# A two-layer mixer with expert retrieval: the context's mixer of layer 0 ahead of the latents', one context expert tile gathered beside the latents' mixer of each layer

## The chip, the cores and the metric

The kernel runs on one core of a Trainium2 chip. The metric is the device time of one execution in microseconds (us); the time before is the median of three runs. All data are float32.

## What is computed

512 latent tokens and 256 context tokens, 1024 wide, pass through two layers. Cut to what matters here:

```
h, hc = modulated RMSNorm of the latents x and of the context xc
p, pc = h @ w_in, hc @ w_in                       # 12 column blocks of q, k, v; z; gates; branches
oc, s_f, s_b = delta rule over pc, both directions, from a zero state
o            = delta rule over p,  both directions, from the context's final states
x = x + gt1 * (concat(o gated by z, 2-D DFT branch, convolution branch) @ w_out)
x = x + gt2 * peer(norm(x))
if not last:                                      # the context is changed in layer 0 only
    xc = xc + cgt1 * (same with oc) ;  xc = xc + cgt2 * peer(norm(xc))

peer(h): 8 heads of product keys choose 16 experts each, 128 for a token;
         y = sum over the 128 of  weight * gelu(u[e] . h) * v[e]
```

The delta rule is worked in chunks of 64 tokens; for each tile a triangular system is solved by an inverse that is doubled level by level.

## The kernel before

Tokens go in tiles of 128, two of context and four of latents; an expert tile is one of them with its 128 slots. A slot is one indirect gather that GpSimd issues: 128 rows of 8 KB (u and v of one expert for each token), 1 MiB. VectorE takes the dot product of u and h, ScalarE gelu, weight and a diagonal matrix, TensorE adds diagonal times v into two PSUM banks (two matmuls for a slot, recorded as four of 512 columns), or VectorE adds weight times v itself.

The stages follow one another, each in a block with one queue of instructions for each engine, ordered by hand:

- Layer 0: `begin` (L153), `projection` (L420, all 768 columns, 18 chunks of weights in a ring of three, 64 dots for the modulation vectors of layer 1 among its VectorE work), `branches` (L1246), `gdn_tiles` (L1426, six tiles), `gdn_scan` (L1788, twelve steps), `mix_out` (L2164, six tiles and the scoring of the first), `peer` (L2455, five tiles: latents, then the first context tile; each tile's successor is scored beside it).
- Layer 1: `projection_latents` (L720), with the last context tile of layer 0 as the held tile (`HeldTile`, L291): all its 128 slots are gathered and summed here through a ring of six rows. Then `branches_beside_context` (L960), which also adds the held sum to the context and projects the context's keys and values, `gdn_tiles` and `gdn_scan` as in layer 0, `mix_out` and `peer` for four tiles.

So ten expert tiles are gathered: nine in `peer`, one held.

Of `gdn_tiles`, for a tile and each of five levels: GpSimd masks a block (L1765), TensorE multiplies (L1549), ScalarE copies (L1633), TensorE multiplies again (L1558, L1561), VectorE subtracts (L1700). The next tile's start (L1658 to L1682) lies between the levels; behind the last level come two passes with the right sides (L1577, L1583) and their copies (L1713). The held tile's methods are called from the queues of a stage: `gathers` on GpSimd (L333), `dve` (dots L347, adds L369), `act` (L376, L379, L386), `pe` (L397). Its ring row is free for slot g + 6 when slot g is summed:

```python
def gathers(self, pool, upto):
    for g in range(self.issued, min(upto, SLOTS)):
        if g >= HELD_RING:
            self.free(pool, g - HELD_RING)
        self.gather(g)
```

In `peer` the same steps are L2585 (gather), L2606 (dot), L2733 to L2741 (ScalarE) and L2831 (TensorE). In `projection`, L524 and L527 are the matmuls of the latents' and the context's columns and L639 the modulation dots; in `projection_latents`, L779 are the latents' columns. In the scoring, L2093 to L2161 pick the experts on VectorE.

Of the kernel before, what the change touches and what calls it, by code (L numbers as in the profile page):

```python
# [10 lines left out]
P = 128  # L11
# [82 lines left out]
def lengths_of(kit):  # L94

    return kit.gw[:, 0, 0:NT * 2 * H].rearrange("p (t g) -> p t g", g=2 * H)
# [48 lines left out]
DOTS_FIRST, DOTS_EACH = 20, 1  # L145
# [7 lines left out]
def begin(nc, kit, hT, spare, ahead):  # L153
# [3 lines left out]
    with ExitStack() as mem, phase(nc, kit, "const_in", "prm_in", "cond_in", "cols_in", "cond_blank", "cond_silu", "cond_ready",  # L157
                                   "prod_ready", "ss_ready", "ms_ready", "root_ready", "xn_ready", "turned", "hT_ready",
                                   "row_copied", "row_turned", "cols_ready", "dve_step", *["x%d" % t for t in range(NT)],
                                   *["w%d" % k for k in range(KD)], in_flight=True) as (  # L160
            const_in, prm_in, cond_in, cols_in, cond_blank, cond_silu, cond_ready, prod_ready, ss_ready, ms_ready, root_ready,
            xn_ready, turned, hT_ready, row_copied, row_turned, cols_ready, dve_step, *ins):
# [18 lines left out]
        with nc.Block() as block:  # L181
            @block.sync
            def _(sp):
# [9 lines left out]
                ahead(sp)  # L193
                sp.wait_ge(prm_in, 16)

            @block.scalar
            def _(act):
# [22 lines left out]
                for k in range(KD):  # L220
                    for st in range(2 if on_act(k) else 0):
                        nc.scalar.activation(hT[:, k, sides[st]], hT[:, k, sides[st]], ACT.Identity,
                                             bias=shift[:, st, k:k + 1], scale=scale[:, st, k:k + 1])
# [30 lines left out]
            def _(dve):  # L254
# [23 lines left out]
                for k in range(KD):  # L278
                    for st in range(0 if on_act(k) else 2):
                        nc.vector.tensor_scalar(hT[:, k, sides[st]], hT[:, k, sides[st]], scale[:, st, k:k + 1],  # L280
                                                shift[:, st, k:k + 1], ALU.mult, ALU.add)
# [4 lines left out]
HELD_A_CHUNK = 6  # L286
HELD_A_ROW = 5
# [3 lines left out]
class HeldTile:  # L291


    BANKS = (1, 3)

    def __init__(self, nc, kit, L, j, sems, rows):
# [4 lines left out]
        self.rows = rows  # L301
        self.h, self.eid, self.gw = kit.hc[:, j % 2, :], kit.eid[:, j % 2, :], kit.gw[:, j % 2, :]
        self.table = kit.experts.rearrange("l e d -> (l e) d")
        TAPS_FROM, TAPS_TO = 6 * HELD_A_CHUNK, 18 * HELD_A_CHUNK
        spare = lambda g: g % 3 == 1 if TAPS_FROM <= g < TAPS_TO else g % 3 != 0
# [47 lines left out]
    def settle(self, dve):  # L353

        for g in range(max(self.dots - 2, 0), self.dots):
            self.add(dve, g)

# [54 lines left out]
PJ_RING = 3  # L412
# [7 lines left out]
def projection(nc, kit, L, first, hT, qkvT, zs, ab, fT, acc, w, w_in):  # L420
# [5 lines left out]
    whole = lambda c: first == 0 or NCV + H <= c < NCV + NQKV  # L426
    segments = lambda c: ((0, CTX), (CTX, T)) if whole(NCV + c) else ((CTX, T),)
    ROWS = SEQ // GRID_W
    W = GRID_W + 2 * HALO
# [3 lines left out]
    with ExitStack() as mem, phase(nc, kit, "mod_in", "mod_prod", "mod_rows", "mod_bias_in", "mod_stored", "wz_in", "proj_ready", "proj_read", "p_ready",  # L433
                                   "y_ready", "y_used", "rows_ready", "padded", "sq_ready", "sum_ready",
                                   "root_ready", "root_turned", "dve_step", "blank", "cond_in", "cond_ready", "dot_bias_in",
                                   "dotted", "dots_biased", "dots_turned", "dots_copied", "dots_stored",
                                   *["dw%d" % r for r in range(DOT_RING)]) as (
            mod_in, mod_prod, mod_rows, mod_bias_in, mod_stored, wz_in, proj_ready, proj_read, p_ready, y_ready, y_used, rows_ready, padded, sq_ready,
            sum_ready, root_ready, root_turned, dve_step, blank, cond_in, cond_ready, dot_bias_in,
            dotted, dots_biased, dots_turned, dots_copied, dots_stored, *dot_w):  # L440
        sb = lambda n, s: mem.enter_context(nc.sbuf_tensor(f"pj{n}_{L}", s, FP32))
        dot_rows = sb("dot", [P, DOT_RING, D])
        next_cols = sb("nx", [P, 2, len(DOTS)])
        next_rows = sb("nr", [P, P])
# [2610 lines left out]
```

## Time and profile before

| | us |
|---|---|
| median of three runs | 4368.07 (4365.26 to 4369.1) |
| span of the profiled execution | 4365.4 |
| layer 0, begin | 44 |
| layer 0, mixer (projection to output) | 628 |
| layer 0, peer, five tiles | 1637 |
| layer 1, mixer up to the scan, with the held tile | 610 |
| layer 1, scan and output | 143 |
| layer 1, peer, four tiles | 1302 |

The profiled execution's span lies 2.7 us below the median of the runs. Over the whole span TensorE is busy for 85%, VectorE 69%, ScalarE 39% and GpSimd 38%, and the DMA engines move 1506 MB. In the rows below, busy times are unions of an engine's instructions; a group's "idle before" is the engine's idle time just before its instructions, with what ended it; the DMA share is the mean busy share of the 16 DMA engines.

### The profile page before, as it was taken

Reading aid. Unit: us, or ns where it says so; the run is one execution under the profiler, and the core shown is the slowest. Engines: PE = TensorE matmul, PEld = TensorE weight load, DVE = VectorE, ACT = ScalarE, POOL = GpSimd, SP = SyncE. Lnnn points to the kernel's source line nnn. Section 1 sums busy time; section 2 is a strip of 40 time slices with the busy share of each in tenths; the row PEclk is TensorE's granted clock in tenths of the full one; section 3 lists DMA queues with packets and bytes.
Section 4 is the critical chain, followed back from the end, with each engine's and each line's share of the span. In section 5 each row is a group of like instructions: output and inputs, shape, how many; then the busy total and the mean of one; then the engine's idle time right before and its main releaser. Section 6 shows DMA issues by size and latency. Waiting matters only on the chain. (4 is left out here: it accounts for less than half of the span.)

```text
span 4365.4 us, 55131 instructions
## 1 busy us (share of the span) xinstructions
PE 3693.1 (85%) x18945; PEld 1903.6 (44%) x18945; DVE 3006.0 (69%) x6251; ACT 1720.2 (39%) x5270; POOL 1645.7 (38%) x1508
## 2 busy tenths in 40 slices
PE   7998998988888887888886888888898888888777
PEld 3566854533433433433432335775443343343222
DVE  3964666975775875875875885557797687687444
ACT  2223623444344344344342454353444433433333
POOL 0004513443443443444443432352444444444332
PEclk9999999999999999999998999899999999999999
DMA  8360159999999999999999997015999999999997
GB/s 336 122 239 29 37 198 367 416 421 421 418 415 422 414 417 421 407 420 422 410 412 369 408 394 303 2 37 190 404 422 421 421 421 421 421 413 421 422 421 325
DMA packets 238985, 1506.07 MB, mean 345 GB/s; under 512 B 28433, under 2 KB 33617, under 8 KB 71153
## 3 DMA queue, kind: packets, MB, share of 16 engines
q0 software_dynamic: 184320, 1342.26, 74.7%
q1 hardware_dynamic: 54384, 160.28, 9.9%
q8 instruction: 150, 2.46, 0.2%
q14 instruction: 131, 1.07, 0.1%
HBM read 1490.32 MB, written 12.12 MB: 344 GB/s over the span
## 5 line engine op out<-in xcount | busy, mean ns | idle before, releaser
L2831 PE MATMUL ps<-low,pediag 128*128 128x512 f32 x2180 | 1058.7, 615 | 226.1 <-ACT pediag L2741 219.3
L2606 DVE CUSTOM_DVE_ANT_0 low<-low,hc 128x1024 f32<-128x1024 f32 x545 | 667.8, 1225 | 359.3 <-DMA low<-in_experts_dram,eid 342.0
L2585 POOL DMA_INDIRECT low<-in_experts_dram,eid x539 | 595.0, 1104 | 812.4 <-PE ps L2831 783.2
L2733 ACT ACTIVATE low<-peact 128x1 f32<-128x1 f32 x1152 | 232.1, 201 | 1335.0 <-DVE peact L2606 1334.0
L2831 PEld LDWEIGHTS ps<-low,pediag 128*128 128x128 f32 x2180 | 388.9, 192 | 824.5 <-ACT pediag L2741 499.4
L2741 ACT ACTIVATE pediag<-cst,low 128x128 f32<-128x128 f32 x1152 | 462.5, 402 | 42.1 <-PE ps L2831 4.5
L2831 PE MATMUL ps<-wide_a,pediag 128*128 128x512 f32 x640 | 307.8, 612 | 54.4 <-ACT pediag L2741 54.2
L2736 ACT ACTIVATE low<-low,gw 128x1 f32<-128x1 f32 x1152 | 339.1, 294 | 37.4
L2831 PE MATMUL ps<-wide_b,pediag 128*128 128x512 f32 x640 | 303.3, 605 | 50.7 <-ACT pediag L2741 48.5
L2060 PEld LDWEIGHTS ps<-qkvT,arena 128*128 128x128 f32 x2560 | 312.0, 193 | 75.4 <-issue 75.4
L2060 PE MATMUL ps<-qkvT,arena 128*128 128x128 f32 x2560 | 313.1, 276 | 2.4 <-ACT qkvT L2024 2.4
L2606 DVE CUSTOM_DVE_ANT_0 wide_a<-wide_a,hc 128x1024 f32<-128x1024 f32 x160 | 196.2, 1226 | 97.3 <-DMA wide_a<-in_experts_dram,eid 91.2
L2606 DVE CUSTOM_DVE_ANT_0 wide_b<-wide_b,hc 128x1024 f32<-128x1024 f32 x160 | 196.2, 1226 | 96.9 <-DMA wide_b<-in_experts_dram,eid 91.4
L2585 POOL DMA_INDIRECT wide_a<-in_experts_dram,eid x158 | 169.8, 1074 | 237.4 <-PE ps L2831 232.7
L2831 PE MATMUL ps<-last_b,pediag 128*128 128x512 f32 x456 | 219.4, 608 | 46.2 <-ACT pediag L2741 44.9
L2831 PE MATMUL ps<-last_a,pediag 128*128 128x512 f32 x456 | 220.5, 612 | 43.0 <-ACT pediag L2741 41.6
L2585 POOL DMA_INDIRECT wide_b<-in_experts_dram,eid x158 | 176.2, 1115 | 195.8 <-PE ps L2831 188.5
L2831 PEld LDWEIGHTS ps<-wide_a,pediag 128*128 128x128 f32 x640 | 114.4, 193 | 227.1 <-ACT pediag L2741 134.8
L2831 PEld LDWEIGHTS ps<-wide_b,pediag 128*128 128x128 f32 x640 | 113.5, 189 | 217.5 <-ACT pediag L2741 120.5
L2606 DVE CUSTOM_DVE_ANT_0 low<-last_b,hc 128x1024 f32<-128x1024 f32 x114 | 139.7, 1225 | 80.9 <-DMA last_b<-in_experts_dram,eid 77.6
L2606 DVE CUSTOM_DVE_ANT_0 low<-last_a,hc 128x1024 f32<-128x1024 f32 x114 | 139.6, 1225 | 76.1 <-DMA last_a<-in_experts_dram,eid 72.2
L2585 POOL DMA_INDIRECT last_b<-in_experts_dram,eid x112 | 121.4, 1084 | 163.1 <-PE ps L2831 156.0
(497 smaller groups left out, 5773.9 us busy)
## 6 DMA issues: line engine op xcount, KB each, us to landing
pjdot<-in_mod_t_dram SPq DMA_DIRECT2D x64, 512.0 KB, 5.2
arena<-in_w_mod_dram SPq DMA_DIRECT2D x24, 1024.0 KB, 14.4
arena<-in_peer_wq_dram SPq DMA_DIRECT2D x8, 2048.0 KB, 17.1
low<-in_experts_dram,eid POOLq DMA_INDIRECT x609, 8.7
pjw<-in_w_cols_dram SPq DMA_DIRECT2D x18, 512.0 KB, 3.7
plw<-in_w_cols_dram SPq DMA_DIRECT2D x18, 512.0 KB, 8.1
x_rows<-low SPq DMA_DIRECT2D x10, 512.0 KB, 7.7
qkvT<-mod_rows SPq DMA_DIRECT2D x9, 512.0 KB, 7.6
```

The costliest lines, as they stand in the source:

```text
L2060: last = self.nc.tensor.matmul(self.kit.ps[:, 4 + q % 2, 0:P], self.kit.wq[:, i, q * P:(q + 1) * P], self.hT[:, i, :], start=i == 0, stop= ...
L2585: nc.gpsimd.indirect_dma_start(ring.row(g), None, table, bass.IndirectOffsetOnAxis(eid[:, j % 2, k:k + 1], 0)).then_inc(ring.landed(g), 16)
L2606: nc.vector.tensor_tensor_reduce(out=dot_out if final else ring.row(g)[:, 0:D], in0=ring.row(g)[:, 0:D], in1=hc[:, j % 2, :], scale=1.0, s ...
L2733: nc.scalar.activation(ge[:, g % 2, 0:1], act_v[:, j % 2, k:k + 1], ACT.Gelu_apprx_tanh).then_inc(gelu_ready, 1)
L2736: nc.scalar.activation(ge[:, g % 2, 1:2], ge[:, g % 2, 0:1], ACT.Copy, scale=gw[:, j % 2, k:k + 1]).then_inc(weighed, 1)
L2741: nc.scalar.activation(diag[:, g % DIAGS, :], ident, ACT.Copy, scale=ge[:, g % 2, 1:2]).then_inc(diag_ready, 1)
L2831: last = nc.tensor.matmul(ps[:, half, :], diag[:, g % DIAGS, :], ring.row(g)[:, D + half * 512:D + (half + 1) * 512], start=k == 0, stop=k ...
```

## The change

1. Layer 0's mixer runs for the context alone first, then for the latents. `projection` becomes `projection_context` (256 columns, eight weight chunks loaded ahead in `begin`, which also stores the latents' turned rows to memory); `branches` becomes `branches_context`; `gdn_tiles` takes a range of tiles, `gdn_scan` a range of steps. The 64 modulation dots (`ModDots`) are spread over these context stages: 6 and 12 in the projection, 14 in the branches, 20 in the delta-rule tiles, 12 in the scan.
2. A new stage `mix_context` makes the output projection of both context tiles, scores all eight heads of context tile 0 and starts its first six gathers.
3. That tile is the held tile of layer 0's latents: 48 slots beside `projection_latents` (two for each of 18 chunks, three for each of four rows of z), 16 beside `branches_latents`, 64 beside `gdn_tiles` (three for each of five levels and one more, for each of four tiles). One slot in three is added on VectorE, the others on TensorE. In `gdn_tiles`, TensorE and ScalarE run one level behind VectorE's dots. `gdn_scan` then does the latents' eight steps, `mix_out` the four latent tiles.
4. `peer` of layer 0 has four tiles; context tile 1 is scored beside the fourth, and its norm's square, turning and store come after the last slot. It is the held tile of layer 1, in the same three stages.
5. In layer 1 the context's rows, keys and values (`context_rows`) and its two delta-rule tiles, without outputs, follow as stages of their own behind the latents' `gdn_tiles`; the scan has twelve steps as before.
6. In `gdn_tiles` the gram and both kinds of differences share PSUM banks 0 and 1 and follow one another, since the held tile's sums take banks 2 and 3.

The core of the diff:

```diff
-DOTS_FIRST, DOTS_EACH = 20, 1
+DOTS_FIRST, DOTS_BRANCHES, DOTS_TILES, DOTS_SCAN = 6, 14, 20, 12
...
 HELD_RING = 6
 HELD_DIAGS = 3
-HELD_A_CHUNK = 6
-HELD_A_ROW = 5
+HELD_BEHIND = 2
+HELD_BRANCHES, HELD_TILE = 16, 16
...
-        spare = lambda g: g % 3 == 1 if TAPS_FROM <= g < TAPS_TO else g % 3 != 0
+        spare = lambda g: g % 3 == 1
...
-PJ_RING = 3
+PJ_RING = 8
...
+def gdn_tiles(nc, kit, L, lo, hi, outs, qk, low, gate, kt, us, wT, qkd, decs, dts, vt, work, held=None, dots=None):
...
+    HELD_LEVEL = 3
...
+            @block.tensor
...
+                for u in range(N):
                     for n in range(NL):
...
+                        if held and u + n:
+                            held.pe(pe, HELD_LEVEL)
+                    if u + 1 < N:
+                        turn_inverse(u + 1)
...
+                    if held:
+                        held.pe(pe, HELD_TILE - NL * HELD_LEVEL)
...
+            @block.scalar
...
+                            elif n == 1:
+                                decay_matrices(u + 1)
+                            elif n == 2:
+                                reach_matrices(u + 1)
                         if n == 3:
+                            decays(u)
+                        if held and u + n:
+                            held.act(act, HELD_LEVEL)
...
+            @block.vector
...
+                            nc.vector.tensor_tensor(both, both, updates(d, kinds), ALU.subtract
                                                     ).then_inc(upd_done, 1)
...
+                        if held:
+                            held.dve(dve, HELD_LEVEL)
+                        if dots:
+                            dots.dve(dve, DOTS_TILES // (N * NL))
...
+            @block.gpsimd
...
+                    if u:
+                        rows_for(HELD_LEVEL)
+                    block_of(u, 2)
+                    right_values(u, 0)
+                    if u:
+                        rows_for(HELD_LEVEL)
+                    block_of(u, 3)
+                    right_keys(u, 0)
+                    rows_for(HELD_LEVEL)
+                    block_of(u, 4)
+                    right_values(u, 1)
+                    rows_for(HELD_LEVEL)
+                    block_of(u, 5)
+                    if u + 1 < N:
+                        block_of(u + 1, 0)
+                    right_keys(u, 1)
+                    rows_for(HELD_TILE - 4 * HELD_LEVEL)
...
+def mix_context(nc, kit, o, mixT, zs, bufs_of, xb, w, held):
...
+                for h in range(PH):
+                    sc.pick(j, 2 * h)
+                    sc.pick(j, 2 * h + 1)
+                    sc.combine(h)
...
+                pool.wait_ge(sc.eid_ready, 1)
+                for g in range(HELD_RING):
...
+                    held.gather(g)
...
-                peer(nc, kit, 0, order, len(order) - 1, qkvT, ring, low[:, LOW_Y:LOW], held)
+            peer(nc, kit, 0, order + [NC - 1], len(order), flat, ring, low[:, LOW_Y:LOW], held)
...
+        context_rows(nc, kit, 1, ctx_qk, ab, gate, yacc, wide, kit.arena[:, PL_ROWS:PL_ROWS + 6 * D])
+        us_c, wT_c, kt_c = solved(PL_ROWS, NC)
+        gdn_tiles(nc, kit, 1, 0, NC, False, ctx_qk, low, gate, kt_c, us_c, wT_c, None, decs, dts, kit.hc[:, 1, :], wide[0])
```

## Rows read from the trace of the kernel before

**Rows 1.** Windows by stage: us, busy us of each engine, TensorE's clock, DMA share, GB/s.

```profile
45.00:300.00 255.00, 254.12 (x877) 150.34 (x877) 195.12 (x322) 45.26 (x83) 2.00 (x7) 0.99 0.57 209
300.00:345.00 45.00, 37.01 (x152) 16.91 (x152) 21.85 (x37) 17.58 (x31) 0.00 (x0) 0.99 0.63 246
345.00:501.00 156.00, 133.42 (x3760) 118.25 (x3760) 82.94 (x122) 58.10 (x171) 84.28 (x73) 0.94 0.01 3
501.00:555.00 54.00, 48.41 (x768) 42.44 (x768) 35.99 (x63) 44.97 (x146) 37.62 (x34) 1.00 0.20 71
...
673.00:2310.00 1637.00, 1386.85 (x4216) 651.56 (x4216) 1189.84 (x2677) 678.92 (x2197) 709.69 (x638) 0.99 1.01 416
2310.00:2690.00 380.00, 304.65 (x708) 135.26 (x708) 295.53 (x418) 161.00 (x410) 145.39 (x128) 0.93 0.96 378
2690.00:2765.00 75.00, 64.88 (x244) 43.79 (x244) 38.85 (x92) 32.10 (x59) 0.23 (x3) 0.90 0.34 127
...
2970.00:3063.00 93.00, 77.47 (x296) 43.84 (x296) 60.70 (x187) 17.70 (x62) 8.90 (x9) 0.92 0.69 256
3063.00:4365.00 1302.00, 1088.56 (x3080) 482.87 (x3080) 891.82 (x1923) 522.29 (x1698) 535.43 (x503) 0.99 0.99 411
```

**Rows 2.** Page, costliest groups: the dot of the expert stages.

```profile
L2606 DVE CUSTOM_DVE_ANT_0 low<-low,hc 128x1024 f32<-128x1024 f32 x545 | 667.8, 1225 | 359.3 <-DMA low<-in_experts_dram,eid 342.0
```

**Rows 3.** Groups by line, 45 to 300 us: columns, dots and their read.

```profile
L639 DVE CUSTOM_DVE_ANT_0 pjdot<-pjdot,hc 128x1024 f32<-128x1024 f32 x64 | 77.8, 1225 | 42.2 <-DMA pjdot<-in_mod_t_dram 30.9 <-ACT hc L601 10.0
L527 PE MATMUL ps<-low,pjw 128*128 128x256 f32 x288 | 65.1, 379 | 0.0
...
L639 DVE DVE_READ_ACCUMULATOR2_ANT pjnx<- 128x1 f32 x64 | 5.3, 82 | 0.0
```

**Rows 4.** Timeline of VectorE, 440 to 466 us: the levels' subtractions in `gdn_tiles`.

```profile
441.94 1.28 DVE L1700 TENSOR_TENSOR gdX<-gdX,ps 128x512 f32<-128x512 f32 x2 [3.21 <-PE ps L1561]
...
447.25 1.27 DVE L1700 TENSOR_TENSOR gdX<-gdX,ps 128x512 f32<-128x512 f32 x2
...
449.99 1.29 DVE L1700 TENSOR_TENSOR gdX<-gdX,ps 128x512 f32<-128x512 f32 x2 [0.87 <-PE ps L1561]
...
460.63 1.39 DVE L1700 TENSOR_TENSOR gdX<-gdX,ps 128x512 f32<-128x512 f32 x2 [0.63 <-PE ps L1561]
465.22 1.28 DVE L1700 TENSOR_TENSOR gdX<-gdX,ps 128x512 f32<-128x512 f32 x2 [3.21 <-PE ps L1561]
```

**Rows 5.** Window of the scoring of four heads in `mix_out`, columns as in Rows 1.

```profile
587.00:635.00 48.00, 47.86 (x201) 28.54 (x200) 40.81 (x142) 6.35 (x19) 2.05 (x2) 1.00 0.33 120
```

**Rows 6.** Held stage: its projection matmuls (by line), one slot's matmuls (timeline).

```profile
L779 PE MATMUL ps<-wide_a,plw 128*128 128x512 f32 x288 | 140.9, 620 | 20.0 <-DMA plw<-in_w_cols_dram 20.0
...
2506.73 1.88 PE L397 MATMUL ps<-low,parts 128*128 128x512 f32 x4
```

**Rows 7.** Line L2450 (first gathers in `mix_out`), from issue to landing.

```profile
DMA to landing us min/median/max: 6.4/6.6/6.9
```

**Rows 8.** Timeline of ScalarE, 2371 to 2378 us: table load, then one held slot.

```profile
2372.61 0.60 ACT L820 ACTIVATE arena<-ps 128x512 f32<-128x512 f32 x1
2373.22 1.28 ACT L376 ACT_TABLE_LOAD   x1
2374.51 0.20 ACT L376 ACTIVATE parts<-parts 128x1 f32<-128x1 f32 x1
2374.75 0.29 ACT L379 ACTIVATE parts<-parts,gw 128x1 f32<-128x1 f32 x1
2375.07 0.40 ACT L386 ACTIVATE parts<-cst,parts 128x128 f32<-128x128 f32 x1
```

**Rows 9.** Lines L1675, L2146, L333: durations min/median/max in ns, first and last start.

```profile
L1675 DVE TENSOR_TENSOR qkd<-qkd,cst x10: 817/1427/1659, 361.9 to 2894.4; 128x512 f32<-128x512 f32 x10
...
L2146 DVE TENSOR_TENSOR qkvT<-qkvT,mosif x8: 691/692/693, 607.5 to 3047.3; 128x512 f32<-128x512 f32 x8
...
L333 POOL DMA_INDIRECT arena<-in_experts_dram,eid x22: 933/940/1986, 2288.6 to 2673.9; - x22
```

More of the change, by code:

```diff
@@ L987, in branches_beside_context @@
-        w = lambda c: wa[:, c] if c < 5 else wb[:, c - 5]
+        gate_c, gain, sc, sh = (room[:, i * D:(i + 1) * D] for i in range(4))
+        xb = room[:, 4 * D:6 * D].rearrange("p (i n) -> p i n", n=D)
+        w = lambda c: weights[c // 4][:, c % 4 * KD * P:(c % 4 + 1) * KD * P].rearrange("p (k n) -> p k n", k=KD)
         hb = kit.hc
@@ L1307, in _ @@
+                dots.load(sp, dots.done + DOT_RING + DOTS_BRANCHES)
+                sp.wait_ge(mod_rows, MOD_GROUPS)
+                for j in range(MOD_GROUPS):
+                    sp.dma_start(mod_store(kit, 0, 2, j), row[32 * j:32 * j + 2, :]).then_inc(mod_stored, 16)
+                sp.wait_ge(mod_stored, 16 * MOD_GROUPS)
             @block.vector
@@ L1795, in gdn_scan @@
     ready_at = {}
-    for c in range(2 * first, NCH):
+    for c in range(S0, s_hi):
         s = max(step_of(d, c // 2, c % 2) for d in range(2))
@@ L2168, in mix_out @@
+def mix_out(nc, kit, L, tiles, o, mixT, flat, zs, w, ring):
     HALVES = 2 * len(tiles)
@@ L2210, in products_reading @@
                 return 1
-            here = [i for i in range(n_tiles) if tiles[i] // 2 == row - 4]
+            here = [i for i in range(n_tiles) if (tiles[i] - NC) // 2 == row - 4]
             return 2 * (max(here) + 1) if here else 1
@@ L2452, in _, with peer @@
                         bass.IndirectOffsetOnAxis(kit.eid[:, 0, g:g + 1], 0)).then_inc(ring.landed(g), 16)
-def peer(nc, kit, L, tiles, here, qkvT, ring, room, held):
+def peer(nc, kit, L, tiles, here, flat, ring, room, held):
     N, M = len(tiles), here
@@ L2961, in backbone @@
[L2961 to L2969 removed]
+        first_row = flat[:, 4 * D:6 * D]
@@ L2972, in constants @@
+        scan.close()
+        with phase(nc, kit, *["e%d" % r for r in range(RING + 2)], gathers=RING + 2) as sems:
+            ring = RowRing(first_row, ring_rows + [kit.cst[:, P:P + 2 * D]], [6, 8, 4, 5, 0, 1, 2, 3, 7], sems[0:RING + 2])
+            mix_out(nc, kit, 1, order, lat_o, lat_mix, flat, lat_z, half_weights, ring)
+            peer(nc, kit, 1, order, len(order), flat, ring, low[:, LOW_Y:LOW], None)
 def constants():
```

1780 lines of the change are left out of this document (986 added, 794 removed).

## The prediction

> **What bounds the kernel now.** I read the stage table first [rows 1]: one row for each stage of the program, with the busy time of each engine, the granted clock and the DMA share. The reader is to see two kinds of stage. In the two expert stages (673 to 2310 us, 3063 to 4365 us) the DMA share is 1.01 and 0.99 while TensorE is busy for 85 and 84%: nine tiles of 128 gathers of 1 MiB go through at 1637/5 = 327 us a tile, 2.55 us a gather. In a mixer stage it is the other way round: TensorE is busy nearly throughout, and the DMA share is 0.01 in layer 0's delta-rule stage and 0.20 in its scan. The one exception is the stage at 2310 us, where a whole expert tile is gathered beside the latents' projection (DMA share 0.96). VectorE's wait for the expert rows [rows 2] is what ends most of its idle time in the expert stages, so an expert tile taken out of them gives back its full price. The question is what the tile costs where it is put, and what it costs to split a mixer stage of six tiles in two.
>
> **What leaves the expert stages.** Layer 0 keeps four tiles in peer instead of five: minus 327. At its end the last context tile gets the norm, the turning and the store that lay beside another tile before, about 14 us with no cover (nothing to 20). Minus 313. Layer 1's expert stage keeps its instructions: 0.
>
> **The context's own mixer in layer 0, stage by stage.** Before, two context tiles ride along with four latent ones; the matmuls are already kept apart by stream, so columns cost the same, but each stage has a start, an end and weights of its own.
> Begin: four stores of the turned latents and five more weight chunks on SP's queue: plus 4 (0 to 8).
> Projection: TensorE alone has 65 us of 256-column matmuls [rows 3], a third of the z pass (15), the modulation products (16) and the wait for the first pieces: 97. VectorE has 18 dots of 1.225 plus 0.08 for the read of the sum [rows 3], 24 us, beside convolutions and taps, at 5.75 us a chunk over twelve chunks. I take 104 (95 to 115).
> Branches: the stage of six tiles lasts 45 [rows 1]; the Fourier products of the latents leave it, 14 dots (18 us of VectorE) and 8 MB of weights come in, at 2.52 us per MiB as in the expert stage 20 us. I take 42 (36 to 48).
> Delta-rule tiles: one tile lasts 23.3 us (441.94 to 465.22 [rows 4]), six of them 140, so 16 of the 156 [rows 1] are start and end. Two tiles: 46.6 + 16 = 63. Two dots (2.6 us) stand behind each of the ten levels' subtractions on VectorE, and the next subtraction queues behind them: the short levels grow from 2.74 us (447.25 to 449.99 [rows 4]) to 3.9, plus 7: 70 (64 to 76).
> Scan: 54 for twelve steps [rows 1], 4.5 a step; four of them 18, with twelve dots (16) and 8 MB of output weights and keys to land: 37 (30 to 42).
> Output and scoring: the held tile needs all 128 expert numbers before its first gathers, so all eight heads are scored with nothing beside them. Four heads take VectorE 40.8 us of 48 [rows 5], eight 82; ahead of them lie the 32 us from 555 to 587, and 5 behind: 119 (112 to 125).
> Sum 104 + 42 + 70 + 37 + 119 = 372, with 4 us between stages 376.
>
> **A held tile beside the latents' mixer, once per layer.**
> Projection with 48 slots: TensorE is busy 304.7 us in the stage of before [rows 1], with 67 slots summed on it and eight context chunks. A slot's four matmuls take 1.88 us in the stream [rows 6], a context chunk 65.1/18 = 3.6 [rows 3]. Two thirds of 48 slots are 32, so 304.7 − 8 × 3.6 − 35 × 1.88 = 210; TensorE sat idle for 20.0 before the first weights [rows 6]: 230 (220 to 245). It is a bound of TensorE, not of the gathers (48 × 2.55 = 122).
> Branches with 16 slots: between the 45 and the 75 that the two stages of before last [rows 1]: 59.
> Delta-rule tiles with 16 slots each: this is the term that decides, and no row of before shows it. Three slots follow each of a tile's five levels on VectorE; TensorE and ScalarE take them one level later; the ring has six rows, so three gathers are issued only when the three of two levels ago are summed. Follow one set of three round: a lone gather lands 6.6 us after its issue [rows 7], the two behind it 2.52 later each, 11.6; the last dot 1.2; gelu, copy and diagonal 0.20 + 0.29 + 0.40 [rows 8]; the matmuls 1.9: 15.6, and with the hand-overs about 16.4 for two levels, 8.2 a level against 2.74 to 5.3 now [rows 4]. Five levels 41; the passes behind the last level 5.2 (23.3 less 4.6 + 5.3 + 3 × 2.74); the sixteenth slot 2.5. ScalarE goes from gelu to exp and back three times a tile, six table loads of 1.28 us [rows 8], 7.7, half of it on the loop: 3.9. Together 53 a tile, 4 × 53 + 16 = 228. From below, a tile can't beat its TensorE work, 133.4/6 = 22.2 [rows 1] + 10.7 × 1.88 = 42, nor 16 gathers, 40: 172 to 184 for the stage. From above, a ring in which each level waits for the set before it (11.5 a level): 245.
> In [rows 8] the table load begins 0.01 us behind the activation ahead of it. The Trainium skill's page "ScalarE: Activation LUTs" (What ACT_TABLE_LOAD costs) adds a drain of about 1.38 us to each switch, 2.66 in all; by it a tile would take 4 us more and the two layers 33. No such gap shows in the rows, so the sum goes without it.
> Sum 230 + 59 + 228 = 517, with gaps 520. The scan of the latents 8 × 4.5 = 36.
>
> **The sums.** Layer 0's mixer: 376 + 520 + 36 + 93 (four tiles of output, as 2970 to 3063 [rows 1]) = 1025 instead of 628 (45 to 673): plus 397, with begin plus 401. Layer 1: 520, then the context's rows, keys and values by themselves (29 of TensorE, 59 with their loads and rows; 45 to 70), two context tiles without outputs (60), 2 of gaps: 641 instead of 610 (2310 to 2920): plus 31. Later stages: 0. Altogether 401 − 313 + 31 = plus 119 on a span of 4365.4, 4484.4. The median of the runs is 2.7 us above the span, so the forecast is 4487, plus 2.7%.
> In other words, splitting costs layer 0 some 220 us (two sets of starts and ends, the scoring that lost its cover), and a held slot costs (517 − 324)/128 = 1.51 us beside the mixer instead of 2.55 in peer; 324 is the same stage without slots (170 + 45 + 109). Gathers are hidden; matmuls, dots and the ring are not.
>
> **Rivals.**
> Faster, by one mechanism: TensorE's slack takes the slots. It is idle for 20 us at the head of the projection and 15% of the delta-rule stage, and its many 64x64 matmuls have modelled ends, so part of "busy" may be room. If a slot costs 0.85 us instead of 1.51, two layers win 256 × 0.66 = 169: 4318 (4280 to 4357 for 0.7 to 1.0). It decides below 1.51 − 119/256 = 1.04 us a slot. Against it: the held tile of before, where nothing else was short, cost (380 − 199)/128 = 1.41 a slot, and TensorE's two thirds alone are 1.25.
> Slower still: VectorE and GpSimd get in each other's way. The same 128x512 product of two SBUF operands takes VectorE 0.69 us where GpSimd does nothing and 0.82 to 1.66 in the delta-rule stages, where GpSimd works; and a gather's issue takes GpSimd 0.93 to 1.99 [rows 9]. Held dots are long operations of that kind, and the block masks that release each level are GpSimd's. If each level's mask waits out one dot (1.2) and three issues grow by 0.3, that is 2.1 for each of 20 levels, 42 a layer: 4487 + 84 = 4571 (4540 to 4640). The Trainium skill's "SBUF — State Buffer" (SBUF: two separate sides) has this as a lock: an operation of VectorE with two SBUF inputs and one of GpSimd that reads SBUF take turns, whole instructions at a time. The stretched rows agree; how often they meet beside a dot no row shows.
> No change: a slot at 1.0 to 1.08. That the gathers do not run beside the mixer at all (2.55 a slot, 4753) speaks against the stage at 2310 us, where they do.
>
> **How the numbers follow.** The forecast with its bounds (4420 to 4540: most of the unknowns are independent, the tiles' 172 to 245 the largest) 0.56; slower still 0.22; faster 0.17; within 0.2%, about what a measurement of this kernel can tell from no change, 0.05. The range leaves out the far ends of both rivals: 4340 to 4580. So faster 0.17, same 0.05, slower 0.78.
>
> **What would show it.** In the changed kernel's trace: layer 0's peer shorter by 313; context stages of about 376 ahead of the latents' projection, with 82 us of scoring on VectorE and a DMA share near 0 there; the delta-rule stages of four tiles at 53 us a tile, VectorE idle for expert rows and GpSimd for sums and adds; the projection of the latents TensorE-bound at 230. Wrong would be tiles of 42 us (the ring covers its latency), or context stages near 300. With both, the change gains.

## The result, and the profile after

The changed kernel takes 4646.2 us (median of four runs, 4639.6 to 4656.4) against 4368.4: 1.064 times the time before, with a 95% interval of 1.062 to 1.065. The direction was forecast, the size was not: plus 278 us instead of plus 119, and past the top of the range.

The profiled execution has a span of 4647.9 us, 282.5 above that of before. Laid out by stage, the answer to [rows 1], windows of the changed kernel (us, busy us of TensorE, its weight loads, VectorE, ScalarE, GpSimd, then TensorE's clock, DMA share, GB/s):

```profile
50.70:162.00 111.30, 99.06 (x436) 72.34 (x437) 69.35 (x141) 24.04 (x51) 0.81 (x6) 0.93 0.70 265
162.00:213.40 51.40, 21.66 (x96) 6.74 (x96) 29.02 (x63) 10.50 (x19) 0.00 (x0) 0.63 0.83 317
213.40:288.40 75.00, 54.17 (x1264) 47.27 (x1264) 55.04 (x82) 20.90 (x60) 33.41 (x25) 0.82 0.44 140
288.40:337.10 48.70, 23.97 (x257) 20.61 (x257) 29.63 (x48) 16.12 (x51) 12.30 (x10) 0.67 0.57 211
337.10:457.30 120.20, 69.12 (x368) 50.70 (x368) 87.92 (x299) 16.64 (x59) 5.82 (x7) 0.77 0.41 153
457.30:721.20 263.90, 231.40 (x568) 107.74 (x568) 144.46 (x212) 107.94 (x216) 54.99 (x52) 0.93 0.67 235
721.20:781.00 59.80, 46.38 (x100) 20.03 (x100) 39.91 (x69) 30.88 (x70) 19.63 (x16) 0.91 0.77 287
781.00:1034.00 253.00, 186.15 (x2680) 116.59 (x2681) 173.42 (x234) 108.67 (x305) 137.32 (x110) 0.88 0.71 257
...
1167.90:2487.90 1320.00, 1114.91 (x3408) 526.66 (x3408) 959.91 (x2172) 547.86 (x1772) 571.30 (x511) 0.98 1.00 414
2487.90:2752.20 264.30, 231.50 (x568) 107.76 (x569) 144.58 (x212) 107.94 (x216) 56.01 (x52) 0.93 0.66 235
...
2811.10:3075.80 264.70, 196.75 (x2680) 120.22 (x2680) 173.22 (x234) 108.64 (x304) 135.69 (x110) 0.84 0.68 247
```

The first five rows are the context's own stages of layer 0 (projection, branches, delta-rule tiles, scan, output with scoring), the next three the latents' stages with the held tile, then layer 0's four expert tiles, then the projection and the delta-rule stage of layer 1. Against the forecast:

| | forecast | measured | off by |
|---|---|---|---|
| begin | +4 | +5.8 | +2 |
| context's stages, layer 0 | 376 | 406.6 | +31 |
| held stages, layer 0 | 520 | 576.7 | +57 |
| scan and output of the latents | 129 | 133.9 | +5 |
| peer, layer 0 | −313 | −317 | −4 |
| held stages, layer 1 | 520 | 587.9 | +68 |
| context's rows and tiles, layer 1 | 121 | 126.5 | +5 |
| scan, output and peer, layer 1 | 0 | 0 | 0 |

Three quarters of the miss lie in the two times three held stages, most of the rest in the context's stages. Inside the held stages the branches came out as forecast (59.8 and 58.9 for 59), though not for the forecast's reasons (a_six below); the projections took 264 each instead of 230 and the delta-rule stages 253 and 265 instead of 228, each with the gap of 2 to 6 us behind it. From first to last instruction, as the stages are timed from here on, they are 262 and 263, 247 and 258.

What the engines wait for in layer 0's delta-rule stage, 781 to 1028 us (engine, line, awaited; us in total, times, longest):

```profile
PE ps L442 <- ACT parts L431: 51.5, 22, 4.7
...
DVE low L414 <- ACT parts L424: 21.9, 10, 5.1
DVE arena L382 <- DMA arena<-in_experts_dram,eid: 13.9, 9, 3.1
...
DVE wide_b L382 <- DMA wide_b<-in_experts_dram,eid: 9.6, 8, 2.0
DVE qkvT L382 <- DMA qkvT<-in_experts_dram,eid: 9.3, 5, 4.4
```

TensorE idles 51.5 us in front of held sums (L442), for their diagonals from ScalarE (L431). VectorE idles 33 us for expert rows and 22 for the weights of its adds. The forecast's loop, in which everything waits for rows, should show the rows first.

There are 22 such waits in the four tiles, of two main kinds. Six of them, 18.6 us together, are like this one; timeline of a level of the changed kernel (start us, duration us, engine, line; "..." stands for lines left out):

```profile
869.66 0.85 ACT L1600 ACTIVATE low<-ps 128x256 f32<-128x256 f32 x2 [4.83 <-PE ps L1502]
...
870.53 1.28 ACT L1574 ACT_TABLE_LOAD   x1
...
871.19 1.28 DVE L1676 TENSOR_TENSOR wide_a<-wide_a,ps 128x512 f32<-128x512 f32 x2 [3.90 <-PE ps L1514]
...
872.45 1.13 PE L1453 MATMUL ps<-low,cst 128*128 128x256 f32 x4
873.62 0.60 ACT L1574 ACTIVATE low<-ps 128x512 f32<-128x512 f32 x1 [1.81 <-PE ps L1453]
874.24 1.28 ACT L421 ACT_TABLE_LOAD   x1
...
876.09 0.40 ACT L431 ACTIVATE parts<-cst,parts 128x128 f32<-128x128 f32 x1
...
876.55 1.98 PE L442 MATMUL ps<-wide_b,parts 128*128 128x512 f32 x4 [2.96 <-ACT parts L431]
...
878.37 1.88 PE L442 MATMUL ps<-arena,parts 128*128 128x512 f32 x4
...
880.18 1.15 PE L1502 MATMUL ps<-wide_a,low 64*64 64x64 f32 x32
```

The subtraction of the level ends at 872.47 and TensorE's matmul for the next tile (L1453) at 873.58; then the next level's first pass (L1502) could start. It starts at 880.18. ScalarE has the next tile's exponential (L1574) ahead of the held slots; the exponential waits for that matmul of TensorE; behind it stands a table load for gelu; and TensorE, whose queue has the held sums ahead of the next pass, waits for the diagonal. The table load begins 0.02 us behind the exponential that ends at 874.22, and the gelu follows at 875.53. The Trainium skill's "ScalarE: Activation LUTs" (What ACT_TABLE_LOAD costs) states a drain of about 1.38 us beside each load; as in [rows 8], no such gap shows here.

The longest wait of each tile is of the other kind (4.2 to 4.7 us, 17.8 us in four):

```profile
829.04 1.28 ACT L1569 ACT_TABLE_LOAD   x1
...
830.34 0.21 ACT L1569 ACTIVATE decs<-gdsums 64x8 f32<-64x8 f32 x1
...
831.71 1.28 ACT L421 ACT_TABLE_LOAD   x1
...
834.44 2.08 PE L442 MATMUL ps<-arena,parts 128*128 128x512 f32 x2 [4.67 <-ACT parts L431]
```

Here ScalarE has eight short exponentials of the tile's own decays (L1569, L1570), which wait for nothing, between two table loads ahead of the held slots. The other 12 waits make 15.1 us.

### The profile page after: what moved, and what is told of

Same layout as the page of the kernel before. It is cut to its first block and busy times, and to the rows that moved or that the text cites. A ratio compares the mean times of both kernels' runs of the same rounds, so it can differ in the third digit from the quotient of the medians.

```text
span 4647.9 us, 55340 instructions
## 1 busy us (share of the span) xinstructions
PE 3748.7 (81%) x18877; PEld 1938.2 (42%) x18877; DVE 3080.5 (66%) x6356; ACT 1825.3 (39%) x5369; POOL 1689.3 (36%) x1513
## 5 line engine op out<-in xcount | busy, mean ns | idle before, releaser
L3047 PE MATMUL ps<-low,pediag 128*128 128x512 f32 x1928 | 921.6, 610 | 180.8 <-ACT pediag L2951 174.7
L3047 PE MATMUL ps<-wide_a,pediag 128*128 128x512 f32 x968 | 471.2, 616 | 97.0 <-ACT pediag L2951 95.2
L3047 PE MATMUL ps<-wide_b,pediag 128*128 128x512 f32 x964 | 465.4, 612 | 89.4 <-ACT pediag L2951 88.7
L2792 POOL DMA_INDIRECT wide_b<-in_experts_dram,eid x237 | 262.1, 1106 | 345.1 <-PE ps L3047 339.2
L2792 POOL DMA_INDIRECT wide_a<-in_experts_dram,eid x238 | 256.7, 1078 | 343.0 <-PE ps L3047 331.7
L741 PE MATMUL ps<-low,wide_a 128*128 128x512 f32 x576 | 266.9, 609 | 67.4 <-DMA low<-h_turned 67.4
L368 POOL DMA_INDIRECT arena<-in_experts_dram,eid x127 | 149.5, 1177 | 305.3 <-PE ps L442 174.5
L442 PE MATMUL ps<-arena,parts 128*128 128x512 f32 x336 | 183.3, 679 | 62.6 <-ACT parts L431 62.5
L382 DVE CUSTOM_DVE_ANT_0 arena<-arena,hc 128x1024 f32<-128x1024 f32 x127 | 170.4, 1355 | 53.4 <-DMA arena<-in_experts_dram,eid 52.4
L741 PEld LDWEIGHTS ps<-low,wide_a 128*128 128x128 f32 x576 | 112.4, 198 | 219.3 <-issue 219.3
```

The costliest lines, as they stand in the source:

```text
L368: self.nc.gpsimd.indirect_dma_start(self.rows[g % HELD_RING], None, self.table, bass.IndirectOffsetOnAxis(self.eid[:, g:g + 1], 0)).then_i ...
L382: self.nc.vector.tensor_tensor_reduce(out=row, in0=row, in1=self.h, scale=1.0, scalar=0.0, op0=ALU.mult, op1=ALU.add, accum_out=self.act_v ...
L442: last = self.nc.tensor.matmul(self.kit.ps[:, b, :], self.diag[:, i % HELD_DIAGS, :], self.rows[g % HELD_RING][:, D + half * 512:D + (half ...
L741: last = nc.tensor.matmul(ps[:, b, :], w[:, c % RING, k, :], hT[:, k, :], start=k == 0, stop=k == KD - 1)
L2792: nc.gpsimd.indirect_dma_start(ring.row(g), None, table, bass.IndirectOffsetOnAxis(eid[:, j % 2, k:k + 1], 0)).then_inc(ring.landed(g), 16)
L3047: last = nc.tensor.matmul(ps[:, half, :], diag[:, g % DIAGS, :], ring.row(g)[:, D + half * 512:D + (half + 1) * 512], start=k == 0, stop=k ...
```

## The experiments

Times are of one run each; the kernel before took 4363.8 to 4376.4 beside them. Stages are read from each run's trace. The changed kernel's own four runs lie 17 us apart, and its two delta-rule stages, which do the same work, 11; one run doesn't show a smaller difference to be real.

**What a slot costs and what the split costs: a_six and b_six.** The changed kernel and the kernel before, with only six slots of a held tile.

```diff
+HELD_N = 6
...
-        for g in range(self.issued, min(upto, SLOTS)):
+        for g in range(self.issued, min(upto, HELD_N)):
...
+        n = max(0, min(n, HELD_N - self.dots))
         for g in range(self.dots, self.dots + n):
```

> The changed kernel with only the first six slots of each of the two held tiles gathered, dotted and summed; 244 slots are left out, everything else stays. It gives the price of a slot beside the mixer and, against the next run, the price of splitting the mixer. If the held slots themselves cost what the trace of the changed kernel suggests (the three held stages last 577 and 588 us against 324 worked out for them without slots, 2.0 us a slot), the time is 4646 - 244 x 2.0, about 4158 us, and the delta-rule stages of four tiles last about 109 us each. If a slot costs the 1.5 us of the prediction and the rest of the miss lies in the stages themselves (their own starts, the lower clock of the context's stages, the shared banks), the time is about 4280 and the delta-rule stages last 150 us without any slot.

> The kernel before with only the first six slots of its one held tile; 122 slots are left out. By the prediction's 1.41 us a slot the time is 4368 - 172 = 4196 us and the latents' projection of layer 1 lasts about 205 us; if that stage was paced by something else than the slots (it stays near 300), about 4290. With the run above: splitting costs (time above) - (this time - 327).

Measured: 4130.0 and 4173.7 us. The latents' projection, branches and delta-rule tiles of layer 0 in the changed kernel without the other slots, windows with columns as above:

```profile
454.00:639.50 185.50, 172.64 (x456) 84.22 (x457) 78.45 (x114) 36.30 (x72) 1.59 (x6) 0.95 0.23 74
639.50:666.80 27.30, 21.93 (x56) 10.07 (x56) 14.13 (x31) 15.16 (x24) 0.00 (x0) 1.00 0.22 77
666.80:778.80 112.00, 93.19 (x2512) 80.82 (x2512) 57.19 (x85) 39.77 (x115) 57.57 (x49) 0.89 0.01 3
```

The delta-rule stage lasts 108 us (109 forecast), so no price of the shared banks and the split tiles shows in it. The three stages together last 325 us with the gaps, for 324, but that sum is luck: the projection took 185 where the forecast had 170, the branches 25 where it had 45. So the miss of the held stages is the slots: (4646 − 4130)/244 = 2.1 us each instead of 1.51; by stage (262.2 us instead of 184.7 for 42 slots, 57.5 instead of 25.2 for 16, 247.5 and 258.5 instead of 108 for 64) 1.8 beside the projection, 2.0 beside the branches and 2.2 to 2.4 beside the delta-rule tiles. The forecast's own terms have 1.25, 0.9 and 1.9: the branches came out at 59 because two errors cancel. In the kernel before a slot cost (4363.8 − 4173.7)/122 = 1.56, where the forecast had 1.41. The split itself: 4130 less (4173.7 − 320 for the expert tile, which is layer 0's peer of b_six, 1637.9, less that of a_six, 1317.9) is 276 us, where the forecast's terms without slots make some 223 (4 for begin, 204 in layer 0, 15 in layer 1).

**Is it the place? c_all_proj.** All 128 slots beside the projection.

```diff
-HELD_BRANCHES, HELD_TILE = 16, 16
+HELD_BRANCHES, HELD_TILE = 0, 0
...
-HELD_CHUNK = 2
-HELD_ROW = 3
+HELD_CHUNK = 6
+HELD_ROW = 5
...
-    HELD_LEVEL = 3
+    HELD_LEVEL = 0
```

> The changed kernel with all 128 slots of each held tile beside the latents' projection (six for each chunk, five for each row of z, as the kernel before has them) and none beside the branches and the delta-rule tiles. If a slot is dear because of where it stands (between the levels of the delta-rule tiles, where TensorE, ScalarE and VectorE each hand work to the next), the projection lasts about 380 us as in the kernel before, the delta-rule stage about 109, and the total falls to about 4550 us. If a slot costs the same 2 us anywhere, the total stays within 20 us of 4646.

Measured: 4529.6, 117 us less. The projection lasts 384 and 383 us, the delta-rule stages 106 and 108, the branches 25. The place counts: 80 slots more cost the projection 122 us, 1.5 each, with a DMA share of 0.94 there.

**VectorE and GpSimd in each other's way: d_one_input.**

```diff
-            self.nc.vector.tensor_tensor_reduce(out=row, in0=row, in1=self.h, scale=1.0, scalar=0.0, op0=ALU.mult,
-                                                op1=ALU.add, accum_out=self.act_v[:, g:g + 1]).then_inc(self.dotted, 1)
+            self.nc.vector.tensor_reduce(out=self.act_v[:, g:g + 1], in_=row, axis=AXX, op=ALU.add).then_inc(self.dotted, 1)
```

> The changed kernel with the held tiles' dot products replaced by a plain sum of the expert row, an operation of VectorE with one SBUF input instead of two; the product with the token is left out, all else stays. If VectorE and GpSimd getting in each other's way is what makes the delta-rule stages dear, the long dots (up to 3.5 us) fall back to 1.2, GpSimd's block masks to 1.28, and the two stages lose about 40 us each: 4565 us. If it is the ring's latency or TensorE waiting behind ScalarE, only the stretch of the dots themselves goes, 15 us a stage at most: 4615 to 4646.

Measured: 4633.0, 13 us less; delta-rule stages 252 and 246. The held dot and the gather's issue (durations min/median/max in ns), first of the changed kernel:

```profile
L382 DVE CUSTOM_DVE_ANT_0 arena<-arena,hc x127: 1212/1224/3533, 460.8 to 3069.6; 128x1024 f32<-128x1024 f32 x127
...
L368 POOL DMA_INDIRECT arena<-in_experts_dram,eid x127: 932/938/1987, 409.2 to 3057.3; - x127
```

and with one SBUF operand:

```profile
L382 DVE TENSOR_REDUCE parts<-arena x127: 1202/1215/1222, 458.4 to 3053.4; 128x1 f32<-128x1024 f32 x127
...
L368 POOL DMA_INDIRECT arena<-in_experts_dram,eid x127: 932/937/1321, 406.9 to 3041.1; - x127
```

The mechanism of the slower rival is there: a dot of 1.22 us takes up to 3.5, and neither it nor the issue is stretched like that once the dot reads one operand. The Trainium skill's "SBUF — State Buffer" (SBUF: two separate sides) states a lock between an operation of VectorE with two SBUF inputs and one of GpSimd that reads SBUF; these rows agree. But the total fell by 13 us, not 84, and 13 is within what the changed kernel's own runs differ by. The rival had three issues grow by 0.3 us a level, and the 60 issues of a delta-rule stage take 73 us instead of 57, 0.27 more each. It also had each level's mask wait out a dot, and there it was wrong: the 24 masks of a stage (L1749) take 33.4 and 33.0 us instead of 30.6 and 31.0.

**Table loads, rows, adds: e_no_gelu, f_ring5, g_all_pe.**

```diff
-... self.ge[:, g:g + 1], self.act_v[:, g:g + 1], ACT.Gelu_apprx_tanh    # e_no_gelu
+... self.ge[:, g:g + 1], self.act_v[:, g:g + 1], ACT.Copy
...
-HELD_RING = 6                                                           # f_ring5
+HELD_RING = 5
...
-        spare = lambda g: g % 3 == 1                                    # g_all_pe
+        spare = lambda g: False
```

> The changed kernel with the held tiles' gelu left out (a plain copy in its place), so that ScalarE never changes its table for a held slot; all else stays. Without slots the delta-rule stage of four tiles lasts 108 us (a_six), with 64 slots 247 and 258, and TensorE idles 51 us of the 247 in front of held sums, behind ScalarE. If the table loads on ScalarE's queue (10 for gelu and 6 or more for exp in that stage, 1.28 us each) are what TensorE waits for, each delta-rule stage loses about 25 us and the projections some 10: total about 4570. If the ring's latency sets the level, ScalarE only waits elsewhere and the total stays above 4625.

> The changed kernel with a ring of five expert rows for the held tiles instead of six. If the round trip of a row (issue, landing, dot, gelu, sum, free) sets the pace of the delta-rule levels, as the prediction's loop had it, the pace goes with the number of rows: 62 us a tile become about 70, 35 us more for each delta-rule stage, and with the other stages the total is 4720 us or more. If TensorE's order behind ScalarE sets it and rows are free in time, the total stays within 20 us of 4646.

> The changed kernel with all held slots summed on TensorE, none added on VectorE (43 sums more for each held tile; its result is the same). If VectorE's adds and their waits for ScalarE (22 us idle and 29 us of adds in the delta-rule stage) stand in the levels' way, each delta-rule stage loses 15 us or more. If TensorE's own time is the bound, 21 slots of 1.9 us make each delta-rule stage 40 us longer, the projections 30 and the total about 4790. A small change either way would say that neither engine but the waiting between them sets the level.

Measured: 4555.2, 4701.8 and 4770.1.

| us | changed | e_no_gelu | f_ring5 | g_all_pe |
|---|---|---|---|---|
| latents' projection, both layers | 262, 263 | 238, 235 | 263, 260 | 295, 297 |
| delta-rule stage, both layers | 247, 258 | 236, 238 | 274, 279 | 272, 272 |

Without gelu each projection loses 25 to 28 us and each delta-rule stage 12 to 21: ScalarE's changes of table were a cost of both, and in the projection a cost that the forecast did not have. TensorE's wait there for diagonals shrinks from the first of these lines (changed kernel, layer 0) to the second:

```profile
PE ps L442 <- ACT parts L431: 20.2, 10, 5.1
...
PE ps L442 <- ACT parts L431: 3.9, 2, 2.3
```

On TensorE, 16 sums more in the projection cost 33 us; 24 of them are TensorE's own busy time, 8 more waits for diagonals. In the delta-rule stage 21 sums more (40 us of TensorE expected) cost 14 to 25. With five rows the stage is 20 to 27 us longer, for 35 expected, and the total lies between the two that were expected: the ring is near its limit, but that doesn't say that it sets the pace with six.

**The ring itself, and the order of the queues: i_no_gather and m_act_order.**

```diff
         for g in range(self.issued, min(upto, SLOTS)):                  # i_no_gather
+            if g >= GATHERED:        # 70
+                self.issued = g + 1
+                continue
...
                                                  ).then_inc(w_copied, 1)   # m_act_order, ScalarE in gdn_tiles
+                        if held and u + n:
+                            held.act(act, HELD_LEVEL)
                         if u + 1 < N:
                             if n == 0:
                                 copy_rows(u + 1)
...
                             decays(u)
-                        if held and u + n:
-                            held.act(act, HELD_LEVEL)
```

> The changed kernel with the gathers of the last 58 slots of each held tile left out: in the delta-rule stages only the first six slots have rows of their own, the others work on the rows that lie in the ring. Dots, gelu, sums and their order stay. Five rows instead of six cost 20 to 27 us a delta-rule stage (f_ring5), so the ring's round trip has some part. If it sets the level, the stages of 247 and 258 us fall to what the engines need, about 190 (TensorE 42 us a tile and start and end): total about 4520. If it is the order of the queues (TensorE behind ScalarE behind the passes), they stay above 235 and the total above 4600.

> The changed kernel with one move in the delta-rule tiles: ScalarE takes the held slots of a level right behind the level's two copies, ahead of the next tile's exponentials and copies instead of behind them. Nothing is left out. TensorE idles 51 us of a 247 us stage in front of held sums whose diagonals stand behind an exponential that itself waits for TensorE. If that order is a part of the price, most of the 51 us goes and each delta-rule stage loses 20 us or more: about 4600. If the ring paces the stage, TensorE then waits elsewhere and the total stays within 15 us of 4646.

Measured: 4635.6 and 4589.7. The delta-rule stages of both layers in the first (windows, then TensorE's first wait in layer 0):

```profile
774.30:1021.80 247.50, 187.28 (x2676) 117.20 (x2677) 158.50 (x229) 107.51 (x302) 68.54 (x51) 0.86 0.05 19
2808.60:3056.14 247.54, 187.22 (x2676) 117.17 (x2677) 158.55 (x229) 107.49 (x302) 68.64 (x51) 0.86 0.05 18
...
PE ps L446 <- ACT parts L435: 49.0, 22, 4.7
```

and in the second:

```profile
777.20:1003.00 225.80, 178.53 (x2676) 113.39 (x2677) 174.66 (x229) 112.21 (x304) 139.04 (x109) 0.89 0.77 289
2784.35:3010.82 226.47, 178.68 (x2680) 113.35 (x2680) 174.10 (x229) 112.49 (x304) 138.42 (x109) 0.90 0.77 286
...
PE ps L442 <- ACT parts L431: 33.5, 22, 4.8
```

This settles the main point. Without a single gather in it (DMA share 0.05) layer 0's stage lasts 247.5 us, as long as with them, and TensorE still waits 49 us for ScalarE; layer 1's lasts 247.5 too, 11 less than with them. With all gathers and one block of instructions moved in ScalarE's queue it lasts 226, in both layers, and the wait falls to 33.5. Most of layer 1's 11 us isn't the ring either, by the changed kernel's two stages as they were:

```profile
781.02:1028.48 247.46, 184.13 (x2676) 115.99 (x2677) 169.62 (x229) 108.14 (x302) 137.31 (x109) 0.88 0.73 263
2811.13:3069.57 258.44, 194.69 (x2676) 119.65 (x2677) 169.42 (x229) 108.14 (x302) 135.66 (x109) 0.83 0.70 253
```

TensorE idles for 63 and 64 us in them. Layer 1's is the longer by its busy time alone, at a lower granted clock (0.83 for 0.88). Without gathers the idle time is 60 us in both layers, with the block moved 47 and 48. So the ring counts for 3 to 4 us of idle time in a stage as it was, the order of the queues for 16, and it is the order that put the level above the forecast. The block was moved ahead of both kinds of exponentials at once, so the runs don't part the two; moving the held sums in TensorE's queue instead wasn't tried.

**What holds the rest: p_order_no_gelu, s_order_no_gather, u_order_one_input.** The moved block together with each of the three earlier edits.

> The mended order of m_act_order with the held gelu left out as in e_no_gelu. If table loads still stand in the levels' way, the delta-rule stages fall from 226 to about 205 us and the total, with the projections' 26 us each, to about 4495. If order was all, the stages stay at 222 or more and the total at 4530 or more.

> The mended order of m_act_order with the last 58 gathers of each held tile left out as in i_no_gather. If the ring's round trip takes over once the order is mended (VectorE idles 19 us for rows in that stage, GpSimd 38 for free rows), the stages fall from 226 to about 200: 4540. If not, they stay within 8 us of 226 and the total within 20 of 4590.

> The mended order of m_act_order with the held dots as sums of one SBUF operand as in d_one_input, where VectorE and GpSimd no longer stretched each other and the total fell by 14 us. If the broken order hid what they cost, each delta-rule stage now falls by 15 us or more: 4560 or less. If they are off the path here too, the total stays within 15 us of 4590.

Measured: 4529.4, 4567.5 and 4566.2. Both delta-rule stages (layer 0, layer 1) by run:

| | us | TensorE busy | idle | clock |
|---|---|---|---|---|
| changed | 247, 258 | 184, 195 | 63, 64 | 0.88, 0.83 |
| e_no_gelu | 236, 238 | 180, 181 | 55, 56 | 0.90, 0.90 |
| i_no_gather | 248, 248 | 187, 187 | 60, 60 | 0.86, 0.86 |
| d_one_input | 252, 246 | 190, 185 | 62, 61 | 0.86, 0.88 |
| m_act_order | 226, 226 | 179, 179 | 47, 48 | 0.89, 0.90 |
| p_order_no_gelu | 227, 221 | 184, 177 | 43, 45 | 0.88, 0.92 |
| s_order_no_gather | 212, 209 | 177, 174 | 35, 35 | 0.90, 0.91 |
| u_order_one_input | 215, 216 | 176, 177 | 39, 39 | 0.90, 0.91 |

The idle time hardly differs between the layers, so it is the steadier measure; busy time times granted clock is 158 to 163 us in every row, and no run shows what moves the clock. The moved block took 16 us of idle time from a stage; the rest of its 22 and 32 us is the busy time at a higher clock. With the order mended, the table loads count 3 to 4 us of idle time instead of 8 (what the total lost, 60 us, is mostly the projections' 26 and 29). Leaving out the gathers now takes 14 to 17 us from a stage, 12 to 13 of them idle, and one operand for the dots 10 to 11, 8 to 9 of them idle; in the order as it was, 3 to 4 and 1 to 2 of idle time. Both totals lie between the two that were expected. The window without gathers:

```profile
778.90:991.00 212.10, 177.22 (x2680) 113.50 (x2680) 166.13 (x230) 110.90 (x304) 74.60 (x51) 0.90 0.05 19
```

TensorE is busy 177 of 212 us, near the lower bound of the forecast (172 to 184), which no run reached. The rest, some 35 us, is TensorE's remaining waits, 24 of them for diagonals; it wasn't taken apart further. A ring of more than six rows wasn't tried.

**The dots: h_short_dots and k_b_short_dots.** The 64 modulation dots cut to 64 columns, in the changed kernel and in the one before.

```diff
-            part = self.ring[:, n % DOT_RING, :]
+            part = self.ring[:, n % DOT_RING, 0:64]
```

> The changed kernel with the 64 modulation dots cut to the first 64 of 1024 columns, loads included (29 MB less); the rest of the products is left out. It shows what the dots cost in the context's stages, where the prediction added about 7 us in the delta-rule tiles, 6 in the branches and 15 in the scan. If the dots are what makes these stages longer than forecast (406 us against 376), the four stages lose about 50 us together: 4596. If the stages are long for their own starts, waits for weights and the lower clock of TensorE there (0.63 to 0.82), they lose less than 25.

> The kernel before with its 64 modulation dots cut to 64 of 1024 columns, loads included, as in h_short_dots, where that took 51 us from the context's four stages of the changed kernel. In the kernel before they lie in the projection of 255 us, of which TensorE is busy 254. If TensorE covers them there, the time stays within 6 us of 4368, and uncovering them is 50 us of what the split costs. If they cost the same there, it falls by 40 or more.

Measured: 4601.9 and 4364.5. In the changed kernel the context's stages fall from 110, 48, 74 and 47 to 96, 36, 63 and 34 us, 51 together (the total by 44). In the kernel before the projection stays as it is:

```profile
44.40:299.70 255.30, 254.43 (x877) 150.52 (x877) 131.24 (x322) 45.37 (x83) 2.10 (x7) 0.99 0.26 85
```

TensorE is busy for 254 of 255 us with VectorE at 131 instead of 195 [rows 1]: there the dots were free. Moved to stages where TensorE is busy for 40 to 90%, they cost 51 us: 37 in the last three of the four, where the forecast had 28 (7, 6 and 15 by the expectation above), and 14 in the projection, where it had 7 at most (104 less TensorE's 97).

## Why the prediction was wrong

Right, by its own steps: that the change is slower and why in outline. An expert tile gives back its price (317 for 313); the context's own mixer costs several hundred us (407), with the scoring uncovered (the stage of 120 us, 119 forecast); the delta-rule tiles without slots last what was worked out (108 for 109; that all three stages without slots do, 325 for 324, is luck); the output, layer 1's context stages and the last expert stage came within 6 us each; and the break-even of about 1 us a slot stands: with the measured terms (276 for the split, 320 for the tile, 190 for the held slots of before) the change would need (320 + 190 − 276)/244 = 0.96 us a slot, below TensorE's share alone (two thirds of 1.88, 1.25).

Of the 164 us by which the span was missed, the delta-rule stages are 62, the projections 68 and the context's stages 31.

The first step that failed is "Follow one set of three round". It took the round trip of an expert row for what sets a level, and put ScalarE and TensorE into it only with their durations. i_no_gather shows that the round trip was not the limit (TensorE's idle time 63 and 64 us with gathers, 60 without), and m_act_order what put the level above the forecast: the place of the held slots in ScalarE's queue, behind exponentials, their table loads and, in a third of the waiting time, a wait for TensorE, while TensorE's queue has the held sums ahead of the next pass. Each of the three queues keeps its order, so a wait of one becomes a wait of the next. The diff printed that order, and the prediction read it for the lag only. It cost 22 and 32 us a stage, 16 of them idle time; with the order mended the 226 us are what was forecast (228), but by then from TensorE's work with smaller waits, not from the loop: that is a coincidence of sizes, and no support for the loop.

The second is the sum for the latents' projection, 304.7 − 8 × 3.6 − 35 × 1.88 = 210 of TensorE's time, and 20 before the first weights. The trace before answers it: matmuls by line, then TensorE's first wait, 2310 to 2690 us:

```profile
L801 PE MATMUL ps<-arena,wide_a 128*128 128x264 f32 x64 | 20.7, 407 | 0.0
L803 PE MATMUL ps<-arena,wide_a 128*128 128x264 f32 x64 | 20.3, 400 | 0.0
L791 PE MATMUL ps<-arena 128*8 128x512 f32 x16 | 8.2, 594 | 0.0
L812 PE MATMUL ps<-cst,arena 8*128 8x8 f32 x8 | 1.1, 254 | 0.0
...
PE ps L397 <- ACT parts L386: 55.7, 30, 4.2
```

With the 288 of L779 [rows 6] and four for each of 67 slots these are all 708 matmuls of the stage [rows 1]: it had no context chunks, and the 28.8 us taken off for them were never in it. And its 380 us are 304.7 busy, 20 at the start and 55.7 in which TensorE waited for diagonals, a term that the forecast put at nothing. A sum cost 2.1 us there, not 1.88: (304.7 − 167.8)/65, with the 167.8 that b_six has with two sums. So 304.7 − 35 × 2.1 = 231, and TensorE was busy for 231. Measured in place of 230 us were 231 busy, 20 waiting for diagonals behind ScalarE's table loads (4 in e_no_gelu) and 12 at the start (457.3 to 468.9). "A bound of TensorE" it is in the main, but not alone.

The third, by size alone, are the context's stages: 31 us, of which the dots are about 16 (51 measured, 35 at most in the forecast). What else is in it wasn't isolated; the granted clock of these stages (0.63 to 0.82 in four of five rows) is a mean between TensorE's two levels of 1.2 and 2.4 GHz, with TensorE idle for half of two of these stages, and lower than in any stage of before [rows 1]; no run separated it from the waits for weights. The "some 220 us" that splitting was to cost layer 0 is 208 by the prediction's own terms (401 less 517 − 324).

The slower rival (4571) came nearest in size and was wrong in cause: its mechanism is real, but worth 13 us in this kernel, no more than its runs differ by, and 24 with the order mended (4589.7 to 4566.2), not 84. The faster rival needed TensorE to have room; its 15% of idle time in the delta-rule stage of before was no room: with slots put there, TensorE's idle time grew from 15 us (a_six) to 63.

No version tried here beats the kernel before. The best of the whole computations, all slots beside the projection, is at 4529.6.

## What to carry to other kernels

When work is slipped into a chain of dependent steps that runs over several engines, go through each engine's queue in order and ask, for the slipped-in instruction, what stands ahead of it and what that waits for: its duration matters less than its place, and moving one block in one queue was worth 56 us here. Idle shares of a latency-bound stage are not room, while a stage in which one engine is busy throughout hides the others' work for nothing (the dots: free in one place, 51 us in the other). Test a supposed pace-setter by taking it away altogether before building on it: fewer rows made the stage slower, yet without any gathers the idle time of its busiest engine was all but the same. And when the time of an old stage is carried over to a new one, add up all of it, busy time and waits, and check that what is taken off was in it.

## What the hardware showed that was not expected

A dot of VectorE can sit out more than one operation of GpSimd, and the next one is stretched in turn; timelines of GpSimd, then VectorE, of the changed kernel:

```profile
904.55 1.28 POOL L1749 TENSOR_TENSOR low<-low,cst 128x512 f32<-128x512 f32 x1
905.78 1.04 POOL L1709 TENSOR_TENSOR low<-cst,low 128x512 f32<-128x512 f32 x1
906.90 1.92 POOL L1714 TENSOR_TENSOR low<-cst,low 128x512 f32<-128x512 f32 x1
...
904.77 3.14 DVE L382 CUSTOM_DVE_ANT_0 wide_b<-wide_b,hc 128x1024 f32<-128x1024 f32 x1 [1.05 <-DMA wide_b<-in_experts_dram,eid]
```

The dot of 1.22 us takes 3.14 and ends 1.1 us behind the second mask; the third takes 1.92 us, where the same mask takes at most 1.38 once the dots read one operand (d_one_input).

And taking the gathers away changed TensorE's idle time in a stage by 3 to 4 us while another wait covered them, and by 12 to 13 once that wait was shorter.
